# The prologue of a two-layer diffusion backbone in another order: filter network first, modulation tiles between its steps, latent stream and its norm next, context last

## The chip, the core and the metric

The kernel runs on one core of a Trainium2 chip: TensorE (PE) multiplies matrices, VectorE (DVE) and ScalarE (ACT) work on tiles, GpSimd (POOL) and SyncE (SP) mostly issue DMA here. Each engine runs its own list of instructions in order, and they meet only at semaphores. The metric is the device time of one execution in microseconds. The kernel before takes 2734.34 us (median of 3 runs, 2731.32 to 2734.46).

## The reference

Two layers over 512 latent tokens and 256 context tokens of width 1024. What matters for the change is the start:

```
m  = (silu(c) @ w_mod[l] + b_mod[l])             # nine vectors of 1024: shift, scale, gate x 3
mc = (silu(c_ctx) @ w_mod[l] + b_mod[l])
h  = rmsnorm(x, g_pre) * (1 + m_scale) + m_shift # adaln_in, before every sub-layer
x  = x + 0.5 * m_gate * rmsnorm(swiglu(h), g_post)
# the same on ctx with mc
# filter of the odd layer's long convolution, for 512 positions:
a  = sin(freq * (z @ f0 + fb0)); a = sin(freq * (a @ f1 + fb1)); a = sin(freq * (a @ f2 + fb2))
k  = (a @ f3) * exp(-t * deltas)                 # forward and backward taps
kf = rfft(concat(k_f, 0, k_b reversed), 2 * 512)
```

The filter depends on no token, so its spectrum is made in the prologue, ahead of the first feed-forward block, and is stored to HBM until layer 1 wants it.

## The kernel before

Everything is held as columns of 128 partitions: x is eight tiles of 128x512, the context eight of 128x256. Weights stream through rings of four blocks `raw`, split on the chip into a high part (`split_hi`, ACT) and a low part (`split_lo`, DVE), and each product takes three matmuls (`three`, L451 to L453): the bulk of the kernel. The first feed-forward block reads h in the same two parts, `h_hi` and `h_lo`.

The order of the work is written out by hand, engine by engine; nothing reorders it. Four strands run in the prologue:

- **The filter network.** `hidden(0..2)`: a matmul on PE (L477), a chain of DVE operations that reduce the argument (L1371 to L1377), a sine on ACT (L904). Then `make_taps`: eight pairs of matmuls (L490), each result multiplied by a decay table `taper` on DVE (L1327); the tables come in a ring of four, issued by SP.
- **The transforms.** `filter_part(0..11)` on PE, four matmuls each (L503), all on tap tiles that `make_taps` must have finished; ACT copies one half out (`copy_odd`, L910), DVE combines the halves (`make_part`, L1338 to L1342). Part n waits until the combination of part n-2 is done. SP stores each finished pair, 1 MB, to HBM.
- **The modulation tiles.** Groups 0 and 1 (shift and scale of the first sub-layer), eight tiles of 512 KB each, through a ring of four issued by POOL: a slot's next load goes out when PE has used it (`mod_units`, L460). `mod_copy` on DVE takes a finished group out of PSUM, `mod_turn` on PE transposes it, `mod_finish` on DVE adds the bias.
- **The norms.** ACT squares tiles (`square_x`), DVE adds them (`add_square`), PE sums over partitions (`norm_sums`), ACT takes the root, DVE inverts (`norm_root`), PE spreads the result over a bank (`norm_spread`).

Last, `adaln_in` makes the eight h tiles. Per tile d: DVE multiplies x by the spread root (`prod`), ACT scales it (`full`) and rounds it (`h_hi`), DVE subtracts (`h_lo`). Between two tiles both engines run a `beside(d)`, with a transform's copy and combination, and at two places a split of weight block 0 or 1. So tile d and a transform are serial with each other: DVE's prod, ACT's full, h_hi and next `copy_odd`, DVE's next `make_part`, DVE's next prod.

Of the kernel before, what the change touches and what calls it, by code (L numbers as in the profile page):

```python
# [25 lines left out]
KT = D // P  # L26
SEQ = 512
CTX = 256
# [19 lines left out]
PAIRS = 8  # L48
# [66 lines left out]
def build(nc, io):  # L115
# [35 lines left out]
    with ExitStack() as ctx:  # L151
# [226 lines left out]
        def _(sp):  # L378
# [5 lines left out]
            for q in range(PAIRS):  # L384
                if q >= 4:
                    sp.wait_ge(taps_ready, 2 * (q - 3))
                sp.dma_start(taper[:, q % 4], io["decay"][q]).then_inc(taper_landed[q % 4], 16)
                if q == 3:
                    sp.dma_start(x[:], io["x"]).then_inc(x_loaded, 16)
                    sp.dma_start(dft_f[:], io["dft_f"]).then_inc(dft_landed, 16)  # L390

            def load_block(b, rel, first, src):
# [49 lines left out]
        def _(pe):  # L442
# [28 lines left out]
            def hidden(layer):  # L471

                if layer == 0:
                    pe.wait_ge(hid_landed, 16 * 3)
                else:
                    pe.wait_ge(hid_ready, layer)
                pe.matmul(psum[:, 0, :], hid_w[:, layer, :], hid[:, :] if layer else pos[:, :],  # L477
                          start=True, stop=True).then_inc(hid_sum, 1)
# [143 lines left out]
            def first_ffns():  # L622

                sx, sc = ffns[0:2]
                at["h"] += KT
                gate_up(sx[0], SEQ)
                down(sx[1], SEQ, HALF_TILES[0])
                gate_up(sx[2], SEQ)
                down(sx[3], SEQ, HALF_TILES[1])
                norm_sums(SEQ, 1)  # L630
                at["h"] += KT
                g = at["group"]

                def beside(i):
                    if i == 0:
                        norm_spread(SEQ)
                    elif i in (1, 2):
                        mod_units(g, range(4 * i - 4, 4 * i))
                    elif i == 4:
                        mod_turn(g)  # L640
                gate_up(sc[0], CTX, beside)
                at["group"] += 1
                norm_sums(SEQ, 0, CTX_STAT)

                def spread(i):
                    if isinstance(i, int) and i == 0:
                        norm_spread(SEQ)
                down(sc[1], CTX, HALF_TILES[0], spread)
                gate_up(sc[2], CTX)
                down(sc[3], CTX, HALF_TILES[1])  # L650
# [1 line left out]
            pe.wait_ge(zeroed, 3)  # L652
            hidden(0)
            pe.wait_ge(c_ready, 1)
            mod_units(0, range(4))
            hidden(1)
            mod_units(0, range(4, 8))
            hidden(2)
            pe.wait_ge(loaded, 16 * LOADS)
            norm_sums(CTX, 1)  # L660
            make_taps(range(4))
            norm_spread(CTX)
            mod_turn(0)
            mod_units(1, range(4))
            make_taps(range(4, PAIRS))
            filter_part(0)
            mod_units(1, range(4, 8))
            filter_part(1)
            filter_part(2)
            mod_turn(1)  # L670
            filter_part(3)
            norm_sums(SEQ, 1)
            filter_part(4)
            norm_spread(SEQ)
            for n in range(5, PARTS):
                filter_part(n)
            at["group"] = 2
            first_ffns()

# [204 lines left out]
        def _(act):  # L884
# [87 lines left out]
            def adaln_in(T, layer, i, who, hi, beside=lambda d: None):  # L972
                for d in range(KT):
                    beside(d)
                    adaln_tile(T, layer, i, who, hi, d)
                at["pre"] += 1
# [57 lines left out]
            for dst, src in ((ident, "ident"), (b_mod, "b_mod"), (g_pre, "g_pre"), (g_post, "g_post"), (rot, "rot"),  # L1034
                             (head_ones, "head_ones"), (sink, "sink"), (ret, "ret")):
                act.dma_start(dst[:], io[src]).then_inc(loaded, 16)
            act.dma_start(cx[:], io["ctx"]).then_inc(ctx_loaded, 16)
            act.wait_ge(zeroed, 3)
            act.wait_ge(c_loaded, 16)
            act.activation(c_silu[:, :, 0:2], c_cols[:], ACT.Silu).then_inc(c_ready, 1)  # L1040
            hidden(0)
            hidden(1)
            act.wait_ge(ctx_loaded, 16)
            square_x(cx, CTX, None)
            hidden(2)
            norm(CTX)
            act.wait_ge(x_loaded, 16)
            for n, tiles in enumerate((range(2), range(2, 5), range(5, 7), range(7, 8))):
                square_x(x, SEQ, None, tiles)
                copy_odd(n)  # L1050
            norm(SEQ)
            copy_odd(4)

            def beside(d):
                if d < 7:
                    copy_odd(5 + d)
                if d in (4, 5):
                    split_hi(d - 4, 0, 1024)
            adaln_in(SEQ, 0, 0, 0, h_hi, beside)
            act.wait_ge(filt_ready, PARTS)  # L1060
            for d in range(3):
                act.wait_ge(filt_stored[d], 32)
# [220 lines left out]
        def _(dve):  # L1283
# [249 lines left out]
            def first_ffns():  # L1533

                sx, sc = ffns[0:2]
                gate_up(sx[0], SEQ)
                down(sx[1], SEQ, False)
                gate_up(sx[2], SEQ)

# [51 lines left out]

            hidden(0)
            hidden(1)
            for d in range(KT - 1):
                add_square(d, CTX, d)
            hidden(2)
            mod_copy(0)
            make_taps(range(PAIRS))
            norm_root(CTX)
            dve.wait_ge(loaded, 16 * LOADS)  # L1600
            make_taps(range(PAIRS, 2 * PAIRS))
            mod_finish(0, 0, 0)
            dve.wait_ge(rbc_ready, 1)
            seq(dve.tensor_copy(kept_rinv[:, 0:CTX], psum[:, RBC, 0:CTX]))
            for n, tiles in enumerate((range(3), range(3, 5), range(5, 7), ())):
                make_part(n)
                for d in tiles:
                    add_square(KT + d, SEQ, d)
                if n == 1:
                    mod_copy(1)  # L1610
            norm_root(SEQ)
            mod_finish(1, 0, 1)
            make_part(4)
            at["group"] += 2
            gain_pre(0, 0)
            at["step"] += 1
            dve.wait_ge(dve_step, at["step"])
            dve.wait_ge(rbc_ready, 2)

            def beside(d):  # L1620
                if d < 7:
                    make_part(5 + d)
                if d in (5, 6):
                    split_lo(d - 5, 0, 1024)
            adaln_in(x, SEQ, h_hi, h_lo, None, beside)
            dve.wait_ge(filt_ready, PARTS)
            first_ffns()

            def split_ahead(b):
# [493 lines left out]
```

## Time and profile before

| what | us |
|---|---|
| median of 3 runs | 2734.34 |
| the profiled execution | 2735.59 |
| its span in the trace | 2733.9 |
| PE busy in the span | 2504.0 |
| first feed-forward matmul starts | 113.67 |
| last transform's combination starts (DVE) | 111.03 |

The profile is one execution. Its page gives busy time for each engine, then the span in slices, then the chain of waits that ended last, and groups of instructions by line.
### The profile page before, as it was taken

How to read it: one execution, taken by the hardware profiler on the slowest of the kernel's cores; microseconds unless marked ns; L12 is line 12 of the kernel's file. 1: busy time of each engine (PE TensorE's matmuls, PEld its weight loads, DVE VectorE, ACT ScalarE, POOL GpSimd, SP SyncE). 2: the span in 40 equal slices, each digit the busy share in tenths (PEclk: the TensorE clock that was granted, in tenths of full speed). 3: DMA queues.
4: the chain of work that ended last, by engine and by line, in shares of the span. 5: the costliest groups of instructions: out<-in, count | busy, mean ns of one | idle time of the engine just before them, and what ended most of it. 6: DMA issues, size and time to landing. Idle time of an engine off the chain costs nothing.

```text
span 2733.9 us, 32899 instructions
## 1 busy us (share of the span) xinstructions
PE 2504.0 (92%) x12514; PEld 1971.3 (72%) x12514; DVE 1209.1 (44%) x1765; ACT 876.5 (32%) x1283; POOL 111.7 (4%) x186
## 2 busy tenths in 40 slices
PE   5899999999899887899999989999989828899997
PEld 2477788899778434778877778778878527788886
DVE  4523233565553676543222353323355385533334
ACT  1422222444431456343222242222244302422222
POOL 1011000000000110000011000100000000000000
PEclk9999999999999899889999989999979969799999
DMA  7566322455312000132356312552212113132322
GB/s 289 196 219 226 128 96 75 151 176 183 130 62 83 31 1 1 62 108 85 100 200 224 130 58 93 193 181 94 91 55 93 70 46 107 49 102 81 108 77 77
DMA packets 91167, 309.53 MB, mean 113 GB/s; under 512 B 10960, under 2 KB 11632, under 8 KB 89776
## 3 DMA queue, kind: packets, MB, share of 16 engines
q1 hardware_dynamic: 67824, 221.75, 24.2%
q0 software_dynamic: 21936, 84.88, 8.7%
q8 instruction: 75, 1.23, 0.2%
q10 hardware_dynamic: 1296, 1.38, 0.1%
q14 instruction: 36, 0.29, 0.0%
HBM read 299.58 MB, written 8.39 MB: 113 GB/s over the span
## 4 chain that ended last, share of the span: by engine, by line
PE 81%; DVE 8%; ACT 4%; DMA 2%; issue 2%; POOLq 0%; POOL 0%; DVEq 0%; ACTq 0%
PE psum L451 24%; PE psum L452 23%; PE psum L453 23%; PE psum L582 2%; DMA mod_raw<-in_w_mod 2%; PE psum L460 2%; PE psum L873 1%; DVE spectrum L359 1%; DVE term L352 1%; PE psum L740 1%; PE psum L604 1%; DVE w_lo L1297 1%; PE psum L862 1%; DVE stats L1767 1%; ACT w_hi L893 0%
## 5 line engine op out<-in xcount | busy, mean ns | idle before, releaser
L451 PE MATMUL psum<-h_hi,w_hi 128*128 128x512 f32 (+1 forms) x2256 | 860.4, 381 | 28.4 <-DVE h_lo L1480 13.7
L452 PE MATMUL psum<-h_lo,w_hi 128*128 128x512 f32 (+1 forms) x2256 | 848.4, 376 | 0.0
L453 PE MATMUL psum<-h_hi,w_lo 128*128 128x512 f32 (+1 forms) x2256 | 847.5, 376 | 0.0
L451 PEld LDWEIGHTS psum<-h_hi,w_hi 128*128 128x128 f32 x2256 | 429.3, 190 | 128.1 <-issue 35.1
L1297 DVE TENSOR_TENSOR w_lo<-raw,w_hi 128x1024 fp32r<-128x1024 f32 (+2 forms) x442 | 470.6, 1100 | 65.3 <-ACT w_hi L893 61.4
L893 ACT ACTIVATE w_hi<-raw 128x1024 fp32r<-128x1024 f32 (+2 forms) x442 | 405.8, 951 | 251.2 <-PE psum L453 243.7
L453 PEld LDWEIGHTS psum<-h_hi,w_lo 128*128 128x128 f32 x2256 | 429.1, 190 | 77.2
L452 PEld LDWEIGHTS psum<-h_lo,w_hi 128*128 128x128 f32 x2256 | 429.8, 191 | 74.0 <-issue 1.0
L451 PE MATMUL psum<-act_hi,w_hi 128*128 128x512 f32 (+1 forms) x880 | 331.5, 377 | 7.5 <-DVE w_lo L1297 5.5
L453 PE MATMUL psum<-act_hi,w_lo 128*128 128x512 f32 (+1 forms) x880 | 329.2, 374 | 0.0
L452 PE MATMUL psum<-act_lo,w_hi 128*128 128x512 f32 (+1 forms) x880 | 329.1, 374 | 0.0
L1391 DVE TENSOR_TENSOR prod<-psum,square 128x512 f32<-128x512 f32 (+1 forms) x110 | 70.2, 638 | 565.5 <-PE psum L453 560.0
L923 ACT ACTIVATE act_hi<-prod 128x512 f32 (+3 forms) x110 | 64.8, 589 | 550.4 <-DVE prod L1391 550.4
L451 PEld LDWEIGHTS psum<-act_hi,w_hi 128*128 128x128 f32 x880 | 166.9, 190 | 44.5 <-issue 13.1
L453 PEld LDWEIGHTS psum<-act_hi,w_lo 128*128 128x128 f32 x880 | 166.8, 190 | 32.0
L452 PEld LDWEIGHTS psum<-act_lo,w_hi 128*128 128x128 f32 x880 | 167.0, 190 | 31.2
L921 ACT ACTIVATE square<-psum 128x512 f32<-128x512 f32 (+1 forms) x110 | 60.7, 552 | 245.2 <-PE psum L453 245.1
L1938 POOL DMA_DIRECT2D mod_raw<-in_w_mod x144 | 76.4, 530 | 1235.0 <-PE psum L460 1095.8
L1434 DVE COPY y<-psum 128x512 f32<-128x512 f32 (+3 forms) x40 | 25.5, 638 | 195.7 <-PE psum L453 195.6
L1396 DVE TENSOR_TENSOR act_lo<-prod,act_hi 128x512 f32 (+3 forms) x110 | 70.3, 639 | 91.7 <-ACT act_hi L923 91.7
L460 PE MATMUL psum<-mod_raw,c_silu 128*32 128x256 f32 x1152 | 82.3, 409 | 27.3 <-DMA mod_raw<-in_w_mod 25.1
L460 PEld LDWEIGHTS psum<-mod_raw,c_silu 128*32 128x32 f32 x1152 | 31.2, 113 | 73.1 <-DMA mod_raw<-in_w_mod 39.6
(229 smaller groups left out, 1812.5 us busy)
## 6 DMA issues: line engine op xcount, KB each, us to landing
raw<-in_gate_up SPq DMA_DIRECT2D x220, 512.0 KB, 4.2
mod_raw<-in_w_mod POOLq DMA_DIRECT2D x144, 512.0 KB, 5.6
raw<-in_down_a SPq DMA_DIRECT2D x80, 384.0 KB, 3.5
raw<-in_down_b SPq DMA_DIRECT2D x80, 320.0 KB, 3.0
raw<-in_hy_in SPq DMA_DIRECT2D x24, 512.0 KB, 3.5
raw<-in_mix_in SPq DMA_DIRECT2D x22, 512.0 KB, 3.5
filt_dram<-made SPq DMA_DIRECT2D x6, 1024.0 KB, 3.8
filt<-filt_dram POOLq DMA_DIRECT2D x2, 3072.0 KB, 10.9
```

The source lines that it names most:

```text
L451: pe.matmul(out, w_hi[:, slot, c:c + P], hi, start=start, stop=False)
L452: pe.matmul(out, w_hi[:, slot, c:c + P], lo, start=False, stop=False)
L453: return pe.matmul(out, w_lo[:, slot, c:c + P], hi, start=False, stop=stop)
L460: ins = pe.matmul(psum[32 * j:32 * j + 32, MODP, 0:256], c_silu[:, k, :], mod_raw[:, k % RING, 256 * j:256 * j + 256], start=(k == 0), sto ...
L582: ins = pe.matmul(psum[:, bank, t:t + 1], src[:, t * P:t * P + P], ones[:, 0:1], start=first and t == 0, stop=last and t == T // P - 1)
L893: act.activation(w_hi[:, slot, 0:cols], raw[:, slot, 0:cols], ACT.Copy).then_inc(hi_split, 1)
L921: act.activation(silu[:, j, 0:T], psum[:, bank, 0:T], ACT.Silu).then_inc(silu_ready, 1)
L923: act.activation(act_hi[:, bass.ds(2 * i + j, 1), 0:T], prod[:, j:j + 1, 0:T], ACT.Copy).then_inc(act_hi_ready, 1)
L1297: ins = dve.tensor_tensor(w_lo[:, slot, 0:cols], raw[:, slot, 0:cols], w_hi[:, slot, 0:cols].bitcast(F32), ALU.subtract)
L1391: ins = dve.tensor_tensor(prod[:, j, 0:T], psum[:, bank, 0:T], silu[:, j, 0:T], ALU.mult)
L1396: dve.tensor_tensor(act_lo[:, fl, 0:T], prod[:, j:j + 1, 0:T], act_hi[:, fl, 0:T].bitcast(F32), ALU.subtract).then_inc(act_ready, 1)
L1938: pool.dma_start(mod_raw[:, k % RING, :], io["w_mod"][layer, v, k]).then_inc(mod_landed[k % RING], 16)
```

## The change

The same operations run in another order in the prologue:

- PE: two modulation tiles, not four, stand ahead of each network layer; the first taps follow directly on the third layer; the other tiles of group 0 stand between tap pairs. The context's norm sums move from ahead of the taps to behind all transforms, and its spread into the first block of the first feed-forward stage. `mod_turn(1)` stands ahead of transform 2 and no longer behind it; the latent norm's sums stand behind transform 2 and not 3.
- ACT: the context's load is issued after the second sine, not at the start; its squares, formerly between the second and third sine, are made one a tile beside the h tiles; the latent squares come as 2, 4, 2 between the copies.
- DVE: the context's additions go beside the h tiles; `mod_copy(1)` follows all seven latent additions. The h tiles stand beside transforms 4 to 11 (before: 5 to 11), and the splits of blocks 0 and 1 one or two tiles earlier.
- SP: x is issued behind the second decay table, not the fourth.

```diff
@@ SP
                 sp.dma_start(taper[:, q % 4], io["decay"][q]).then_inc(taper_landed[q % 4], 16)
+                if q == 1:
+                    sp.dma_start(x[:], io["x"]).then_inc(x_loaded, 16)
                 if q == 3:
-                    sp.dma_start(x[:], io["x"]).then_inc(x_loaded, 16)
                     sp.dma_start(dft_f[:], io["dft_f"]).then_inc(dft_landed, 16)
@@ PE, first feed-forward stage and prologue
+                def spread_ctx(i):
+                    if isinstance(i, int) and i == 0:
+                        norm_spread(CTX)
+                gate_up(sx[0], SEQ, spread_ctx)
-            mod_units(0, range(4))
+            mod_units(0, range(2))
             hidden(1)
-            mod_units(0, range(4, 8))
+            mod_units(0, range(2, 4))
             hidden(2)
+            make_taps(range(2))
+            mod_units(0, range(4, 6))
+            make_taps(range(2, 4))
+            mod_units(0, range(6, 8))
+            make_taps(range(4, 6))
             pe.wait_ge(loaded, 16 * LOADS)
-            norm_sums(CTX, 1)
-            make_taps(range(4))
-            norm_spread(CTX)
             mod_turn(0)
             mod_units(1, range(4))
-            make_taps(range(4, PAIRS))
+            make_taps(range(6, PAIRS))
             filter_part(0)
             mod_units(1, range(4, 8))
             filter_part(1)
+            mod_turn(1)
             filter_part(2)
-            mod_turn(1)
+            norm_sums(SEQ, 1)
             filter_part(3)
-            norm_sums(SEQ, 1)
-            filter_part(4)
             norm_spread(SEQ)
-            for n in range(5, PARTS):
+            for n in range(4, PARTS):
                 filter_part(n)
+            norm_sums(CTX, 1)
@@ ACT
-            act.wait_ge(ctx_loaded, 16)
-            square_x(cx, CTX, None)
+            act.dma_start(cx[:], io["ctx"]).then_inc(ctx_loaded, 16)
             hidden(2)
-            norm(CTX)
...
             def beside(d):
-                if d < 7:
-                    copy_odd(5 + d)
-                if d in (4, 5):
-                    split_hi(d - 4, 0, 1024)
+                copy_odd(4 + d)
+                square_x(cx, CTX, None, range(d, d + 1))
+                if d in (2, 3):
+                    split_hi(d - 2, 0, 1024)
             adaln_in(SEQ, 0, 0, 0, h_hi, beside)
+            norm(CTX)
@@ DVE
-            for n, tiles in enumerate((range(3), range(3, 5), range(5, 7), ())):
+            for n, tiles in enumerate((range(4), range(4, 7))):
                 make_part(n)
                 for d in tiles:
-                    add_square(KT + d, SEQ, d)
-                if n == 1:
-                    mod_copy(1)
+                    add_square(d, SEQ, d)
+            mod_copy(1)
+            make_part(2)
             norm_root(SEQ)
...
             def beside(d):
-                if d < 7:
-                    make_part(5 + d)
-                if d in (5, 6):
-                    split_lo(d - 5, 0, 1024)
+                if d < KT:
+                    make_part(4 + d)
+                if d in (3, 4):
+                    split_lo(d - 3, 0, 1024)
+                if 1 <= d < KT:
+                    add_square(KT + d - 1, CTX, d - 1)
```

Where that puts things. TensorE's list, from the second network layer to the transforms (L477, L478: network layer; L460, L461: modulation tiles; L490, L491: taps; L503, L504: transforms), before:

```order
L477 MATMUL psum<-hid,hid_w 128x512
L460 MATMUL psum<-mod_raw,c_silu 32x256 x16
L477 MATMUL psum<-hid,hid_w 128x512
L582 MATMUL psum<-ones,sumsq 128x1 x2
L582 MATMUL psum<-ones,square 128x1 x2
L490 MATMUL psum<-f,hid 128x512 x8
L604 MATMUL psum<-ident,full 128x128 x2
L468 MATMUL psum<-ident,mod_row 128x128 x2
```

and now:

```order
L478 MATMUL psum<-hid,hid_w 128x512
L461 MATMUL psum<-mod_raw,c_silu 32x256 x8
L478 MATMUL psum<-hid,hid_w 128x512
L491 MATMUL psum<-f,hid 128x512 x4
L461 MATMUL psum<-mod_raw,c_silu 32x256 x8
L491 MATMUL psum<-f,hid 128x512 x4
L461 MATMUL psum<-mod_raw,c_silu 32x256 x8
```

Two modulation tiles (x8) stand between the layers where four (x16) stood, and the context's sums (L582) and spread (L604) are gone from here.

VectorE's list around transform 1, from its combination (L1338 and L1342, now L1344 and L1348) on; L1414 and L1420 add squares, L1309 and L1315 are `mod_copy(1)`, which TensorE's `mod_turn(1)` waits for. Before:

```order
L1338 TENSOR_TENSOR made<-psum,raw 128x512
L1342 SCALAR_TENSOR_TENSOR made<-psum,raw 128x512
L1414 TENSOR_TENSOR sumsq<-sumsq,square 128x512 x2
L1309 COPY mod_row<-psum 128x256
L1338 TENSOR_TENSOR made<-psum,raw 128x512
```

and now:

```order
L1344 TENSOR_TENSOR made<-psum,raw 128x512
L1348 SCALAR_TENSOR_TENSOR made<-psum,raw 128x512
L1420 TENSOR_TENSOR sumsq<-sumsq,square 128x512 x3
L1315 COPY mod_row<-psum 128x256
L1344 TENSOR_TENSOR made<-psum,raw 128x512
```

Three additions stand ahead of the copy where two stood.

VectorE's list beside two h tiles that have no split, before:

```order
L1338 TENSOR_TENSOR made<-psum,raw 128x512
L1340 TENSOR_TENSOR made<-psum,raw 128x512
L1476 TENSOR_TENSOR prod<-x,psum 128x512
L1480 TENSOR_TENSOR h_lo<-full,h_hi 128x512
L1338 TENSOR_TENSOR made<-psum,raw 128x512
```

and now:

```order
L1344 TENSOR_TENSOR made<-psum,raw 128x512
L1346 TENSOR_TENSOR made<-psum,raw 128x512
L1420 TENSOR_TENSOR sumsq<-sumsq,square 128x256
L1482 TENSOR_TENSOR prod<-x,psum 128x512
L1486 TENSOR_TENSOR h_lo<-full,h_hi 128x512
L1344 TENSOR_TENSOR made<-psum,raw 128x512
```

One addition of 128x256, of the context's squares, now stands between the combination and the next tile's prod.

## Rows read from the trace of the kernel before

**Rows 1.** Part 1 of the page: busy us, share, instructions.

```profile
PE 2504.0 (92%) x12514; PEld 1971.3 (72%) x12514; DVE 1209.1 (44%) x1765; ACT 876.5 (32%) x1283; POOL 111.7 (4%) x186
```

**Rows 2.** Chain of waits near its first matmul: start us, us, what.

```profile
111.03 0.69 DVE made L1338
...
112.32 1.15 DVE w_lo L1297
```

**Rows 3.** Timeline of TensorE, prologue: start us, us, line, tiles, idle before.

```profile
15.38 1.08 PE L460 MATMUL psum<-mod_raw,c_silu 128*32 128x256 f32 x8 [1.53 <-DMA mod_raw<-in_w_mod]
16.39 2.08 PE L477 MATMUL psum<-hid,hid_w 128*128 128x512 f32 x2
...
31.60 1.08 PE L460 MATMUL psum<-mod_raw,c_silu 128*32 128x256 f32 x8 [1.31 <-DMA mod_raw<-in_w_mod]
32.61 2.08 PE L477 MATMUL psum<-hid,hid_w 128*128 128x512 f32 x2
...
39.90 6.26 PE L490 MATMUL psum<-f,hid 64*128 64x512 f32 x16 [4.32 <-ACT hid L904]
...
58.94 3.67 PE L503 MATMUL psum<-taps,dft_f 128*128 128x512 f32 x8 [1.46 <-DVE taps L1327]
62.55 1.93 PE L460 MATMUL psum<-mod_raw,c_silu 128*32 128x256 f32 x32
64.41 7.13 PE L503 MATMUL psum<-taps,dft_f 128*128 128x512 f32 x16
71.92 0.44 PE L468 MATMUL psum<-ident,mod_row 128*128 128x128 f32 x2 [0.38 <-DVE mod_row L1309]
...
75.63 0.95 PE L582 MATMUL psum<-ones,sumsq 128*128 128x1 f32 x8
...
77.33 3.68 PE L503 MATMUL psum<-taps,dft_f 128*128 128x512 f32 x8
80.85 1.05 PE L604 MATMUL psum<-ident,full 128*128 128x128 f32 x8
81.74 17.34 PE L503 MATMUL psum<-taps,dft_f 128*128 128x512 f32 x40
...
113.67 0.76 PE L451 MATMUL psum<-h_hi,w_hi 128*128 128x512 f32 x1 [6.66 <-DVE w_lo L1297]
...
126.15 1.93 PE L460 MATMUL psum<-mod_raw,c_silu 128*32 128x256 f32 x32
```

**Rows 4.** Timeline of ScalarE: a network layer's sine, the first split after the filter.

```profile
11.61 0.63 ACT L904 ACTIVATE hid<-hid_arg_t 128x512 f32<-128x512 f32 x1 [2.35 <-DVE hid_arg_t L1377]
...
121.35 2.01 ACT L893 ACTIVATE w_hi<-raw 128x1024 fp32r<-128x1024 f32 x2 [4.42 <-DMA filt_dram<-made]
```

**Rows 5.** Windows: busy us by engine, granted clock, DMA share, GB/s.

```profile
12.00:17.00 5.00, 2.70 (x17) 0.90 (x18) 0.00 (x0) 0.23 (x1) 0.97 (x2) 1.00 1.04 416
...
114.00:116.00 2.00, 2.00 (x6) 1.52 (x6) 1.66 (x4) 1.88 (x3) 0.00 (x0) 0.50 0.96 252
1070.00:1080.00 10.00, 6.26 (x46) 3.94 (x48) 7.54 (x18) 5.45 (x11) 0.00 (x0) 1.00 0.01 2
```

**Rows 6.** Timeline of VectorE, prologue.

```profile
53.81 4.99 DVE L1327 TENSOR_TENSOR taps<-psum,taper 128x512 f32<-128x512 f32 x8 [5.61 <-PE psum L490]
...
68.85 0.69 DVE L1338 TENSOR_TENSOR made<-psum,raw 128x512 f32<-128x512 f32 x1 [2.25 <-ACT raw L910]
...
71.45 0.42 DVE L1309 COPY mod_row<-psum 128x256 f32<-128x256 f32 x1
...
86.10 0.69 DVE L1338 TENSOR_TENSOR made<-psum,raw 128x512 f32<-128x512 f32 x1 [2.92 <-ACT raw L910]
...
90.07 0.69 DVE L1338 TENSOR_TENSOR made<-psum,raw 128x512 f32<-128x512 f32 x1 [2.08 <-issue]
...
111.03 0.69 DVE L1338 TENSOR_TENSOR made<-psum,raw 128x512 f32<-128x512 f32 x1 [1.48 <-issue]
```

**Rows 7.** VectorE groups by shape: busy us, mean ns.

```profile
L1414 DVE TENSOR_TENSOR sumsq<-sumsq,square 128x256 f32<-128x256 f32 x6 | 2.5, 425 | 0.6
```

More of the change, by code:

```diff
@@ L625, in first_ffns @@
                 at["h"] += KT
-                gate_up(sx[0], SEQ)
+                def spread_ctx(i):
+                    if isinstance(i, int) and i == 0:
+                        norm_spread(CTX)
+                gate_up(sx[0], SEQ, spread_ctx)
                 down(sx[1], SEQ, HALF_TILES[0])
@@ L1036, in _ @@
                 act.dma_start(dst[:], io[src]).then_inc(loaded, 16)
-            act.dma_start(cx[:], io["ctx"]).then_inc(ctx_loaded, 16)
             act.wait_ge(zeroed, 3)
@@ L1042, in _ @@
             hidden(1)
-            act.wait_ge(ctx_loaded, 16)
-            square_x(cx, CTX, None)
+            act.dma_start(cx[:], io["ctx"]).then_inc(ctx_loaded, 16)
             hidden(2)
-            norm(CTX)
             act.wait_ge(x_loaded, 16)
-            for n, tiles in enumerate((range(2), range(2, 5), range(5, 7), range(7, 8))):
+            for n, tiles in enumerate((range(2), range(2, 6), range(6, 8))):
                 square_x(x, SEQ, None, tiles)
@@ L1051, in _ @@
             norm(SEQ)
-            copy_odd(4)
+            copy_odd(3)
+            act.wait_ge(ctx_loaded, 16)
             def beside(d):
-                if d < 7:
-                    copy_odd(5 + d)
-                if d in (4, 5):
-                    split_hi(d - 4, 0, 1024)
+                copy_odd(4 + d)
+                square_x(cx, CTX, None, range(d, d + 1))
+                if d in (2, 3):
+                    split_hi(d - 2, 0, 1024)
             adaln_in(SEQ, 0, 0, 0, h_hi, beside)
+            norm(CTX)
             act.wait_ge(filt_ready, PARTS)
@@ L1535, in first_ffns, with keep_ctx @@
                 sx, sc = ffns[0:2]
-                gate_up(sx[0], SEQ)
+                def keep_ctx(i, j):
+                    if isinstance(i, int) and i == 0 and j == 1:
+                        dve.wait_ge(rbc_ready, 2)
+                        seq(dve.tensor_copy(kept_rinv[:, 0:CTX], psum[:, RBC, 0:CTX]))
+                gate_up(sx[0], SEQ, keep_ctx)
                 down(sx[1], SEQ, False)
@@ L1593, in _ @@
             hidden(1)
-            for d in range(KT - 1):
-                add_square(d, CTX, d)
             hidden(2)
+            make_taps(range(10))
             mod_copy(0)
-            make_taps(range(PAIRS))
-            norm_root(CTX)
+            make_taps(range(10, 2 * PAIRS))
             dve.wait_ge(loaded, 16 * LOADS)
-            make_taps(range(PAIRS, 2 * PAIRS))
             mod_finish(0, 0, 0)
-            dve.wait_ge(rbc_ready, 1)
-            seq(dve.tensor_copy(kept_rinv[:, 0:CTX], psum[:, RBC, 0:CTX]))
-            for n, tiles in enumerate((range(3), range(3, 5), range(5, 7), ())):
+            for n, tiles in enumerate((range(4), range(4, 7))):
                 make_part(n)
                 for d in tiles:
-                    add_square(KT + d, SEQ, d)
-                if n == 1:
-                    mod_copy(1)
+                    add_square(d, SEQ, d)
+            mod_copy(1)
+            make_part(2)
             norm_root(SEQ)
             mod_finish(1, 0, 1)
-            make_part(4)
             at["group"] += 2
             gain_pre(0, 0)
+            make_part(3)
             at["step"] += 1
             dve.wait_ge(dve_step, at["step"])
-            dve.wait_ge(rbc_ready, 2)
+            dve.wait_ge(rbc_ready, 1)
             def beside(d):
-                if d < 7:
-                    make_part(5 + d)
-                if d in (5, 6):
-                    split_lo(d - 5, 0, 1024)
+                if d < KT:
[4 more added lines that the diff above has]
+                    add_square(KT + d - 1, CTX, d - 1)
             adaln_in(x, SEQ, h_hi, h_lo, None, beside)
             dve.wait_ge(filt_ready, PARTS)
+            norm_root(CTX)
             first_ffns()
```

## The prediction

> **What bounds the kernel now.** I read the page's engine totals first, then the chain of waits, then the timelines of TensorE, VectorE and ScalarE over the first 126 us. The totals say that TensorE is busy for 92% of the span [rows 1], so what the change can give is what it takes from the time before TensorE's steady work, or adds to it. The change touches only that stretch: the first feed-forward matmul stands at 113.67 us, after 6.66 us in which TensorE waited for VectorE [rows 3], and the chain of waits runs back from it through the split of block 1 into the combination of the last transform at 111.03 [rows 2]. Behind the first pair of blocks comes the list of before, so each microsecond by which that matmul comes earlier is a microsecond of the kernel, as long as nothing that it needs later is late.
>
> Four pieces set the 113.67. (a) The filter network: layer 1 enters TensorE at 16.39 and layer 2 at 32.61, both behind modulation tiles that waited for their DMA (the tiles before them are at 15.38 and 31.60), and taps start at 39.90 [rows 3]. (b) Taps until the first transform, 39.90 to 58.94 [rows 3]. (c) Transforms 0 to 4, TensorE almost without a gap, until transform 5 at 81.74 [rows 3]. (d) A loop between ScalarE and VectorE: the combination of transform 5 starts at 86.10 and of transform 6 at 90.07, the last at 111.03 [rows 6]. One transform of TensorE lasts about 3.5 us (81.74 plus 17.34 for five) [rows 3], the loop's step 3.97, so here TensorE waits for VectorE.
>
> **(a) The network, cheaper by 13.0 us.** Layer 0's sine ends at 11.61 + 0.63 = 12.24 [rows 4]. Only tiles 0 and 1 stand ahead of layer 1 now, so it enters at 12.3. From a layer's matmul to what follows it takes 39.90 - 32.61 = 7.3 us [rows 3]: layer 2 enters at 19.6. Tiles 2 and 3 in between ended at 15.38 + 1.08 = 16.46 [rows 3] and hide. Taps start at 26.9, against 39.90.
>
> **(b) Taps, to transform 0 at 44.6 (before 58.94).** TensorE starts them after some 5 us of idling. The window behind the wait before the first feed-forward matmul shows the granted clock at 0.50, the level of 1.2 GHz, after 6.66 us idle [rows 3, 5]; eight tap matmuls (four pairs) took 6.26 us from 39.90 [rows 3] with such a start, 1.6 us a pair. I take 1.7 us for each of the first two pairs and half of that later: pairs 0 and 1 until 30.3, tiles 4 and 5 until 31.4, pairs 2 and 3 and tiles 6 and 7 until 34.1. What ends last is the DMA of group 1. Its first four tiles can only go out as slots come free, at 31 to 34, and decay tables 4 to 7 go out as VectorE uses 0 to 3, from 30. That is 8 x 0.5 MB at 416 GB/s, the rate of a full window [rows 5]: about 10 us, until 40.5 or 41. Then pairs 6 and 7 until 42.7, and VectorE's last multiplications at 4.99 / 8 = 0.62 us each [rows 6] until 44.5. If no tile were late it would be 42.7; with 3 us more of DMA, 47.5. I keep both ends. The decay tables 2 and 3 now stand behind x in SP's list; they have until 32 to land, and x and they are part of the bytes already counted.
>
> **(c) Transforms 0 to 3 and the norm, dearer by 6.** Transform 0 until 48.2 (62.55 - 58.94 = 3.6), four tiles until 50.1 (64.41 - 62.55), transform 1 until 53.65 (3.55 each from the pair of 7.13) [rows 3]. Then TensorE stands before `mod_turn(1)`. Before, transform 1 ended at 67.97 under transform 2, its combination began at 68.85, and the copy at 71.45 was through at 71.87 [rows 6], 3.9 us after; the wait in front of the turn was 0.38 because transform 2 covered it [rows 3]. Now that cover is gone, and a third addition, at the 0.75 us of an addition and a squaring that wait for each other (estimate from the 68.85 and 71.45 rows: 2.60 less 1.20 of combination, over two), makes it 4.65: the turn is at 58.3, transform 2 at 58.6. Queued behind that wait is all of TensorE's list. After an idle stretch of that length I expect the clock at 1.2 GHz again; the first seven feed-forward matmuls after 113.67 ran at 0.50 [rows 5], about 3 us that cost 1.5. Transform 2 ends at 58.6 + 3.5 + 1.5 = 63.6. Bounds of the clock's part: 0, and 3.0 if it falls twice (the stretch before transform 0 is also thin). Then the sums (77.33 - 75.63 = 1.7), transform 3 (80.85 - 77.33 = 3.5) and the spread (81.74 - 80.85 = 0.9) [rows 3], until 69.7. The square root's table must now be loaded here; it falls under transform 3 with its inversion and costs nothing, 3.5 us of cover. From the end of the spread to the combination that opens the loop it was 86.10 - 81.74 = 4.36 [rows 3, 6]: 74.05, 12.05 earlier than 86.10.
>
> **(d) The loop, dearer by 7.4.** Before: six steps in 111.03 - 86.10 = 24.93 [rows 6], five of 3.97 and one with a split in it, 1.13 longer. (The second split came behind the last combination.) Now seven steps: 7 x 3.97 = 27.8; both splits inside, 2.26; and in six of them an addition of the context's squares, which lies between VectorE's combination and prod, so in the loop. It lasts 425 ns [rows 7]; as VectorE's instructions overlap by some 50 ns, 0.38 each, 2.3 together. Sum 32.3: the last combination starts at 106.35, against 111.03. ScalarE's squares and first splits stand where it waits for prod and cost nothing. TensorE needs 3.5 us for a transform and has a step of 4.35, so it does not set the pace.
>
> **The end.** Before, 111.03 to 113.67 is 2.64: combination 1.2, split 1.13, the rest issue [rows 2, 3]. Now the split is gone, and the last context addition (0.38) and `norm_sums(CTX)` stand there, which last half of the 1.7 of the latent ones, at 1.2 GHz perhaps 1.0 in all: 106.35 + 1.2 + 0.4 + 1.0 + 0.15 = 109.1. That is 4.6 earlier. The context's spread now falls into TensorE's full work, two matmuls of the four that took 0.9 [rows 3]: +0.45. What is late next are weight blocks 2 and 3, whose slots the transforms use and whose split waits for the last store: 121.35 was 9.1 us after the last combination's end [rows 2, 4], so 116.7 now, and 3.2 us of splits make it 119.9; the pair of blocks 0 and 1 lasts 126.15 - 113.67 = 12.5 [rows 3] until 121.6. Covered by 1.7, and modulation tiles come between.
>
> **The sum.** -13.0 (a), -1.3 (b, 19.0 to 17.7), +2.3 (c and the transform taken out of it: 27.16 from transform 0 to the loop before, 29.45 now), +7.4 (d), end 0.1, spread +0.45: -4.1 us. The profiled execution took 2735.59, which gives 2731.5; it lies 1.25 above the median of 2734.34, so against that the forecast is 2730.2, 0.15% less. A difference under 0.2%, 5.5 us, is what a measurement here can't tell from none.
>
> **Rivals.**
> 1. *The stall of (c) is smaller or the clock holds.* For it: TensorE has only idled about 4.65 us there, and where DMA lands quickly transform 0 can start at 42.7. Against it: the 0.50 window above. With both, 1.5 + 1.9 more: -7.5, 2726.8.
> 2. *The tiles are late.* Everything in (b) hangs on 4 MB issued in one burst from 30 us on, and tiles 4 to 7 of group 1 have only 7 us. Price: 3 us at transform 0 or in front of transform 1: -1.1, 2733.2. Against it: tables and tiles are what the first 27 us have already loaded at full rate.
> 3. *Slower: TensorE's clock falls in the loop.* The transforms now meet a gap of 0.9 us in each step and of 2.0 in the two with a split; at 1.2 GHz a transform lasts 7 us, more than a step, and TensorE sets the pace. From transform 5 at 73.2, seven of them would end at 122.2 and the first feed-forward matmul would stand at 124.6: +10.9 and the spread, +11.4, 2745.7. It decides from the point at which the low clock lasts for more than four transforms (up to there TensorE's lead covers it). Against it: at 1070 to 1080 us TensorE was busy for 6.26 of 10 us and the granted clock was 1.00 [rows 5]. The Trainium skill, "TensorE: Matmul & The Clock Gate", section "A second HAM failure mode: psum-queue depth-cycling", says that small idle gaps between groups of matmuls, as PSUM banks are cycled, can make the clock swing between its levels; this kernel's loop is of that kind, and by that rule alone this rival would be the forecast. The row at 1070 us speaks against the rule here.
>
> **How the numbers follow.** Forecast 0.60, rival 1 0.18, rival 2 0.12, rival 3 and its half-way forms 0.10. The forecast's own spread, from the ends of (b) (-1.9, +3) and of the clock (-1.5, +1.5), is 2727 to 2734; a good third of it is beyond 5.5 us. So faster 0.60 x 0.37 + 0.18 = 0.40, within 0.2% 0.60 x 0.63 + 0.12 = 0.50, slower 0.10. The range goes to 2725.5 for rival 1 with a run spread of 1.5 us, and to 2735.5 for rival 2 likewise.
>
> **What the changed profile would show.** Layer 1 on TensorE at about 12.3 and layer 2 at 19.6; taps at 26.9; transform 0 at 44.6 behind a DMA wait on modulation tiles; a wait of about 4.65 us before L469 for VectorE's mod_row, and a window of 0.50 after it; the loop's combinations 4.35 us apart (5.5 with a split); the first L452 at 109.1; L605 inside the first stage. A transform 0 after 48, a step over 5 us without a split, or blocks 2 and 3 waited for would make the forecast wrong; so would a stall that transform 2 somehow covers.

## The result: slower by 4.5 us, where 4.1 us less was forecast

| | before | changed |
|---|---|---|
| median, us | 2734.46 (9 runs) | 2738.97 (9 runs) |
| lowest to highest | 2728.05 to 2736.39 | 2737.59 to 2744.85 |
| span of the profiled execution | 2733.9 | 2736.4 |
| first network matmul on TensorE | 5.11 | 4.99 |
| first feed-forward matmul | 113.67 | 118.52 |

The ratio is 1.0022, 95% interval 1.0013 to 1.0031: small, but the interval doesn't reach 1. Single runs of either kernel scatter by 7 or 8 us, so the traces are compared by a mark that the scatter of the rest doesn't touch: the time from the first network matmul to the first feed-forward matmul. It was 108.56 us and is 113.53, 5.0 more, and the medians lie 4.5 apart.

### The profile page after: what moved, and what is told of

The parts are those of the page before. It is cut to its first block, busy times and chain, and to the rows that moved or that the text cites. A ratio compares the mean times of both kernels' runs of the same rounds, so it can differ in the third digit from the quotient of the medians.

```text
span 2736.4 us, 32902 instructions
## 1 busy us (share of the span) xinstructions
PE 2506.0 (92%) x12514; PEld 1971.2 (72%) x12514; DVE 1209.5 (44%) x1765; ACT 875.7 (32%) x1283; POOL 111.7 (4%) x186
## 4 chain that ended last, share of the span: by engine, by line
PE 81%; DVE 8%; ACT 4%; issue 2%; DMA 1%; DVEq 0%; POOLq 0%; POOL 0%; ACTq 0%
PE psum L452 24%; PE psum L453 24%; PE psum L454 24%; PE psum L583 2%; PE psum L461 2%; DMA mod_raw<-in_w_mod 1%; PE psum L880 1%; DVE spectrum L359 1%; DVE term L352 1%; PE psum L747 1%; PE psum L605 1%; PE psum L869 1%; DVE stats L1776 1%; DVE w_lo L1303 0%; ACT w_hi L900 0%
## 5 line engine op out<-in xcount | busy, mean ns | idle before, releaser
L454 PEld LDWEIGHTS psum<-act_hi,w_lo 128*128 128x128 f32 x880 | 166.0, 189 | 31.9
L453 PEld LDWEIGHTS psum<-act_lo,w_hi 128*128 128x128 f32 x880 | 166.1, 189 | 31.3
L1440 DVE COPY y<-psum 128x512 f32<-128x512 f32 (+3 forms) x40 | 25.5, 638 | 195.6 <-PE psum L454 195.6
L461 PE MATMUL psum<-mod_raw,c_silu 128*32 128x256 f32 x1152 | 80.4, 402 | 16.6 <-DMA mod_raw<-in_w_mod 14.4
L880 PE MATMUL psum<-idft,spectrum 128*128 128x256 f32 x128 | 32.1, 418 | 56.0 <-DVE spectrum L359 56.0
```

Source lines behind the costliest of these rows:

```text
L453: pe.matmul(out, w_hi[:, slot, c:c + P], lo, start=False, stop=False)
L454: return pe.matmul(out, w_lo[:, slot, c:c + P], hi, start=False, stop=stop)
L880: ins = pe.matmul(psum[:, 4 + n % 2, i * HB:i * HB + HB], y_f[c][:, i, m, t * P:t * P + P], idft[:, m, :], start=(m == 0), stop=(m == 3))
```

## The profile after

The total work of TensorE is nearly the same, 2506.0 us against 2504.0 [rows 1]:

```profile
PE 2506.0 (92%) x12514; PEld 1971.2 (72%) x12514; DVE 1209.5 (44%) x1765; ACT 875.7 (32%) x1283; POOL 111.7 (4%) x186
```

TensorE's timeline of the changed kernel, columns as in [rows 3]. L478 is the network, L491 taps, L461 modulation tiles, L504 transforms, L469 `mod_turn`, L583 and L605 a norm's sums and spread:

```profile
12.16 2.07 PE L478 MATMUL psum<-hid,hid_w 128*128 128x512 f32 x2 [1.05 <-ACT hid L911]
...
19.36 1.32 PE L478 MATMUL psum<-hid,hid_w 128*128 128x512 f32 x2 [3.05 <-ACT hid L911]
25.90 3.79 PE L491 MATMUL psum<-f,hid 64*128 64x512 f32 x8 [5.22 <-ACT hid L911]
...
33.90 1.99 PE L491 MATMUL psum<-f,hid 64*128 64x512 f32 x8
...
45.15 1.08 PE L461 MATMUL psum<-mod_raw,c_silu 128*32 128x256 f32 x8 [1.42 <-DMA mod_raw<-in_w_mod]
46.16 3.79 PE L491 MATMUL psum<-f,hid 64*128 64x512 f32 x8
51.41 5.10 PE L504 MATMUL psum<-taps,dft_f 128*128 128x512 f32 x8 [1.47 <-DVE taps L1333]
56.44 1.93 PE L461 MATMUL psum<-mod_raw,c_silu 128*32 128x256 f32 x32
58.31 3.70 PE L504 MATMUL psum<-taps,dft_f 128*128 128x512 f32 x8
66.62 0.69 PE L469 MATMUL psum<-ident,mod_row 128*128 128x128 f32 x2 [4.61 <-DVE mod_row L1315]
67.10 5.72 PE L504 MATMUL psum<-taps,dft_f 128*128 128x512 f32 x8
72.66 0.95 PE L583 MATMUL psum<-ones,sumsq 128*128 128x1 f32 x8
...
77.88 1.05 PE L605 MATMUL psum<-ident,full 128*128 128x128 f32 x8
78.77 17.61 PE L504 MATMUL psum<-taps,dft_f 128*128 128x512 f32 x40
...
116.79 1.01 PE L583 MATMUL psum<-ones,sumsq 128*128 128x1 f32 x4 [5.24 <-DVE sumsq L1420]
...
118.52 0.77 PE L452 MATMUL psum<-h_hi,w_hi 128*128 128x512 f32 x1
```

The second and third layers enter at 12.16 and 19.36 and the taps at 25.90, where the forecast had 12.3, 19.6 and 26.9: the 13 us are there (39.90 - 25.90 = 14.0). From 37 us on TensorE waits for one tile of group 1 after another, and uses the fourth at 45.15. The last two tap pairs, forecast to be over at 42.7, start at 46.16 and take 3.79 us, where two pairs at full clock take 1.99 (at 33.90), and transform 0 takes 5.10 instead of 3.67 [rows 3]. It starts at 51.41, 7.5 us before the 58.94 of before: half of the gain is gone there, and the wait that follows takes most of the rest. At 66.62 stands the wait for `mod_row` that the forecast had at 4.65 us: 4.61. Transform 2 behind it takes 5.72.

VectorE, the combinations of transforms 1, 4, 6, 7 and 11 (L1344) and the copy behind the additions (L1315), to be read beside [rows 6]:

```profile
62.74 0.69 DVE L1344 TENSOR_TENSOR made<-psum,raw 128x512 f32<-128x512 f32 x1 [1.49 <-ACT raw L917]
...
66.14 0.42 DVE L1315 COPY mod_row<-psum 128x256 f32<-128x256 f32 x1
...
83.18 0.69 DVE L1344 TENSOR_TENSOR made<-psum,raw 128x512 f32<-128x512 f32 x1 [3.12 <-ACT raw L917]
...
91.33 0.69 DVE L1344 TENSOR_TENSOR made<-psum,raw 128x512 f32<-128x512 f32 x1 [1.48 <-issue]
...
95.63 0.69 DVE L1344 TENSOR_TENSOR made<-psum,raw 128x512 f32<-128x512 f32 x1 [1.48 <-issue]
...
115.11 0.69 DVE L1344 TENSOR_TENSOR made<-psum,raw 128x512 f32<-128x512 f32 x1 [1.48 <-issue]
```

From the combination at 62.74 to the copy at 66.14 it is 3.4 us (2.6 before, one addition less). The step at 91.33 to 95.63 is 4.30 (3.97 before), the loop 115.11 - 83.18 = 31.93 (32.3 forecast).

Five windows of the changed kernel; the last three columns are granted clock, DMA share and GB/s:

```profile
20.00:30.00 10.00, 4.78 (x14) 1.47 (x16) 5.77 (x10) 1.67 (x3) 0.00 (x0) 0.51 1.00 414
30.00:36.00 6.00, 5.88 (x48) 2.10 (x40) 4.40 (x8) 0.00 (x0) 2.11 (x4) 0.97 0.90 298
40.00:50.00 10.00, 6.02 (x28) 1.59 (x24) 1.31 (x3) 0.00 (x0) 1.68 (x4) 0.53 1.02 397
68.00:72.00 4.00, 4.00 (x7) 1.69 (x6) 0.00 (x0) 0.00 (x0) 0.00 (x0) 0.58 0.09 37
100.00:110.00 10.00, 6.53 (x15) 2.50 (x14) 6.78 (x11) 4.73 (x9) 0.00 (x0) 1.00 0.17 70
```

The clock is at 0.51 and 0.53 in the two stretches in which TensorE waits for the network and for tiles, while the DMA engines are full; it is at 0.58 in transform 2; and at 1.00 in the loop, where TensorE is busy for 6.5 of 10 us. So the third rival's fall of the clock did not come. The Trainium skill ("TensorE: Matmul & The Clock Gate", section "A second HAM failure mode: psum-queue depth-cycling") reports of a bf16 kernel that small gaps between groups of matmuls, as PSUM banks are cycled, made the clock swing. This trace does not agree: its fp32 transforms go round four banks too, with gaps of 0.6 to 1.74 us in front of the last three, and the granted clock stays at 1.00.

POOL's issues of group 1's first four tiles, each pair when TensorE has used the slots:

```profile
31.31 1.19 POOL L1947 DMA_DIRECT2D mod_raw<-in_w_mod  x2 [13.79 <-PE psum L461]
34.21 1.19 POOL L1947 DMA_DIRECT2D mod_raw<-in_w_mod  x2 [1.71 <-PE psum L461]
```

They go out at 31.31 to 34.9, as forecast ("at 31 to 34"). The fourth lands 10.2 us later, at 45.1, where the forecast had 41. Between 30 and 36 us the DMA engines are busy (0.90) but move only 298 GB/s, not the 416 that the forecast counted with, and from 31.3 to 45.15 they move 5.1 MB (13.84 us at 371 GB/s), not the 4 that it counted: weight blocks 0 and 1 and the next tiles go out in between.

ScalarE's split of blocks 2 and 3 came at 125.66 against 121.35 [rows 4], the same distance behind the last combination, and was not waited for, as forecast.

## The experiments

All but the last are edits of the changed kernel. "The mark" is the first feed-forward matmul minus the first network matmul in the profiled execution. Each ratio is to the kernel before as timed beside that run, so ratios compare better than medians.

| run | mark, us | median, us | ratio to before, 95% |
|---|---|---|---|
| before | 108.56 | | |
| changed | 113.53 | 2738.97 | 1.0022 [1.0013, 1.0031] |
| turn_behind | 108.80 | 2738.23 | 1.0011 [0.9995, 1.0027] |
| taps_first | 106.86 | 2733.45 | 0.9999 [0.9986, 1.0012] |
| adds_aside | 110.86 | 2740.59 | 1.0012 [0.9996, 1.0028] |
| raw_late | 111.95 | 2735.67 | 1.0013 [1.0000, 1.0026] |
| tiles_early | 105.37 | 2730.65 | 0.9998 [0.9987, 1.0008] |
| filler | 110.17 | (one run) 2736.46 | |
| three | 104.62 | 2730.27 | 0.9995 [0.9985, 1.0006] |
| copy_only | 106.59 | 2732.48 | 0.9988 [0.9977, 1.0000] |
| copy_ahead | 93.07 | 2719.89 | 0.9963 [0.9949, 0.9976] |
| before_copy (edit of before) | 103.61 | 2729.74 | 0.9985 [0.9971, 0.9999] |

**tiles_early: why the tiles were late.**

```diff
             hidden(2)
+            mod_units(0, range(4, 6))
             make_taps(range(2))
-            mod_units(0, range(4, 6))
-            make_taps(range(2, 4))
             mod_units(0, range(6, 8))
+            make_taps(range(2, 4))
             make_taps(range(4, 6))
```

> The changed kernel with tiles 4 and 5 of modulation group 0 used right behind the third network layer (TensorE waits there for 5.2 us anyway) and tiles 6 and 7 behind tap pair 1, so that the ring's slots come free for group 1 some 7 us earlier (they went out at 31.31 to 35.4). Theory G (group 1 was late because its slots came free late): its fourth tile is used at 38 to 40 and no longer at 45.15, and the first feed-forward matmul comes 5 to 6 us earlier. Theory H (the DMA engines were full, so the bytes that had to be moved by then set the time): they were at 0.84 to 0.96 only from 30 to 36 us, so the fourth tile comes 1 to 2 us earlier at most.

POOL's issues for group 1 and TensorE's rows:

```profile
24.07 0.53 POOL L1947 DMA_DIRECT2D mod_raw<-in_w_mod  x1 [5.76 <-PE psum L461]
27.70 0.53 POOL L1947 DMA_DIRECT2D mod_raw<-in_w_mod  x1 [3.10 <-PE psum L461]
33.06 0.53 POOL L1947 DMA_DIRECT2D mod_raw<-in_w_mod  x1 [4.84 <-PE psum L461]
33.90 0.53 POOL L1947 DMA_DIRECT2D mod_raw<-in_w_mod  x1 [0.31 <-issue]
```

```profile
22.31 1.08 PE L461 MATMUL psum<-mod_raw,c_silu 128*32 128x256 f32 x8
25.94 1.08 PE L461 MATMUL psum<-mod_raw,c_silu 128*32 128x256 f32 x8 [2.55 <-DMA mod_raw<-in_w_mod]
...
38.98 1.93 PE L461 MATMUL psum<-mod_raw,c_silu 128*32 128x256 f32 x32
...
44.64 3.67 PE L504 MATMUL psum<-taps,dft_f 128*128 128x512 f32 x8 [1.80 <-DVE taps L1333]
```

A window of this run:

```profile
30.00:36.00 6.00, 5.39 (x30) 1.38 (x28) 3.94 (x7) 0.00 (x0) 1.05 (x2) 1.00 0.99 403
```

Tiles 4 and 5 of group 0 were there at 22.31 and 25.94, inside TensorE's wait for the network; the changed kernel used them only at 29.62. The first two tiles of group 1 go out at 24.07 and 27.70 and not at 31.31 and 32.0, and at 38.98 all four are used in one piece (x32) without a wait. The fourth is through 5.3 us earlier (6.2 counted from the first network matmul), transform 0 starts at 44.64, and the mark falls by 8.2, to 3.2 under that of the kernel before. The clock gives 3.2 of the 8.2: it is high again for the last tap pairs (1.99) and transform 0 (3.67). Theory G holds: late slots made the tiles late. But the fourth tile's own slot was hardly late: it goes out at 33.90, 1 us earlier than in the changed kernel, and lands in 5.9 us instead of 10.2. What the edit took away are two of the loads that stood with it in the burst, and the DMA engines move 403 GB/s from 30 to 36 us instead of 298. Whether the smaller burst or the higher rate counts for more isn't told apart.

**raw_late: were it the bytes?**

```diff
+            sp.wait_ge(filt_ready, 1)
             def load_block(b, rel, first, src):
```

> The changed kernel with the loads of weight blocks 0 and 1 (1 MB) held until the first transform's combination is done; they were issued at 35 to 37 us, in the middle of the burst of decay tables and modulation tiles. Theory A (the bytes of that burst set the landing): 1 MB less at 416 GB/s makes the fourth tile of group 1 land 2.4 us earlier, at 42.7, and all behind it. Rival F (the tiles wait for their ring slots, not for bytes): tile 4 stays at 45.15.

```profile
45.60 1.08 PE L463 MATMUL psum<-mod_raw,c_silu 128*32 128x256 f32 x8 [0.46 <-DMA mod_raw<-in_w_mod]
...
51.43 3.67 PE L506 MATMUL psum<-taps,dft_f 128*128 128x512 f32 x8 [1.47 <-DVE taps L1335]
```

The fourth tile is still used at 45.60; theory A's 42.7 failed. It went out 1.4 us later in this run and landed in 9.3 us instead of 10.2, so holding back that 1 MB gave about 1 us. (From 30 to 36 us the DMA engines moved even less than in the changed kernel, 223 GB/s; why the rate falls there stays open.) The mark's 1.6 comes from a transform 0 at full clock (3.67). Together with tiles_early: what counted was when the tiles went out and what went out with them, not the weight blocks.

**taps_first: what stood behind the tiles.**

```diff
-            mod_units(1, range(4))
             make_taps(range(6, PAIRS))
+            mod_units(1, range(4))
             filter_part(0)
```

> The changed kernel with tap pairs 6 and 7 ahead of the first four tiles of modulation group 1 on TensorE, not behind them. In the changed kernel TensorE waited for those tiles until 45.15, ran the two pairs at a half clock until 49.95, and transform 0 started at 51.41. Theory A (late tiles in front of the last taps): transform 0 starts as soon as the fourth tile is used, at 46.2, so 5 us earlier, and the first feed-forward matmul at 113.3. Rival D (the tiles are not what is late but the decay tables of those pairs): transform 0 stays at 50 or later.

```profile
45.71 0.64 PE L461 MATMUL psum<-mod_raw,c_silu 128*32 128x256 f32 x8 [1.70 <-DMA mod_raw<-in_w_mod]
46.28 3.70 PE L504 MATMUL psum<-taps,dft_f 128*128 128x512 f32 x8
```

The tile is as late as before (45.71), yet transform 0 starts at 46.28, as theory A had it, and the mark falls by 6.7. Both kernels use the tile at about the same time; what is spared is the two tap pairs and VectorE's multiplications behind it, 5.1 us. The rest is the clock (transforms 0 and 2 take 3.70 and 4.76 us, not 5.10 and 5.72), less 1.1 us at the last tile of group 1, which is late in its turn.

**turn_behind: the wait for the copy.**

```diff
             filter_part(1)
-            mod_turn(1)
             filter_part(2)
+            mod_turn(1)
```

> The changed kernel with mod_turn(1) behind transform 2 again, as before the change; nothing else. Its first feed-forward matmul stood at 118.52 us, after a wait of 4.61 us in front of that turn and a transform 2 of 5.72 us at a half clock. Theory A (the gain of the network was spent on three waits ahead of the loop: late tiles, this turn, and the clock that both lower): the wait goes and transform 2 takes about 3.7, so the first feed-forward matmul comes 6 to 7 us earlier, near 112, and the kernel 6 us. Rival B (the loop beside the h tiles alone sets the end, whatever comes ahead of it): it stays within 1 us of 118.5. Rival C (only the clock counts, the wait moves to another place behind transform 1): 2 us earlier.

```profile
58.55 7.13 PE L504 MATMUL psum<-taps,dft_f 128*128 128x512 f32 x16
66.86 0.44 PE L469 MATMUL psum<-ident,mod_row 128*128 128x128 f32 x2 [1.17 <-DVE mod_row L1315]
...
68.83 5.38 PE L504 MATMUL psum<-taps,dft_f 128*128 128x512 f32 x8
```

Transform 2 covers the wait, 1.17 us of it are left, and the mark falls by 4.7. That is less than the 6 to 7 expected: transforms 1 and 2 run at full clock (7.13 for both), but now transform 3 takes 5.38. The low clock has moved behind the norm's sums. From transform 1 to transform 4 this run needs 16.4 us and the changed kernel 20.5: 4.1 us are the edit's. The rest of the 4.7 is transform 0, at full clock here, less tiles that came somewhat later. By their ratios to the kernel before (1.0011 and 1.0022) the two differ by 3 us, within their intervals.

**filler: the clock by itself.**

```diff
+            for _ in range(4):
+                pe.matmul(psum[:, STAT, :], dft_f[:, 0, 0, 0, :], taps[0][:, 0, :], start=True, stop=True)
             mod_turn(1)
```

> The changed kernel with four spare matmuls of a transform's shape (3.4 us, into a bank that nothing reads) in front of mod_turn(1), so that TensorE waits 1.2 us there and not 4.61. It gives the clock's part alone: theory A (the low clock after the wait costs about 2 us in transform 2): transform 2 takes 3.7 and not 5.72, and the first feed-forward matmul comes 2 us earlier although the turn is at the same time. Rival: transform 2 stays at 5 or more, the clock doesn't follow the wait.

```profile
60.91 3.60 PE L677 MATMUL psum<-taps,dft_f 128*128 128x512 f32 x8
65.67 0.44 PE L469 MATMUL psum<-ident,mod_row 128*128 128x128 f32 x2 [1.17 <-DVE mod_row L1317]
65.95 3.60 PE L504 MATMUL psum<-taps,dft_f 128*128 128x512 f32 x8
```

The turn comes no sooner (65.67 - 57.37 from the start of transform 1, 8.30 as in the changed kernel), but transform 2 takes 3.60. From its start to the sums it is 3.44, against 5.56: the low clock cost 2.1 us there, where the forecast had 1.5. That is one pair of profiles: in the five other runs that keep this wait in front of transform 2 (taps_first, adds_aside, raw_late, tiles_early, copy_only), the transform took 4.76 to 6.17 us, so the cost is 1.2 to 2.6. The mark falls by 3.4; the rest is transform 0, at full clock in this run.

**adds_aside: the additions in the loop.**

```diff
-                if 1 <= d < KT:
+                if d == KT - 1:
                     add_square(KT + d - 1, CTX, d - 1)
-            adaln_in(x, SEQ, h_hi, h_lo, None, beside)
+            for d in range(KT + 1):
+                beside(d)
+                adaln_tile(x, SEQ, h_hi, h_lo, psum[:, RBC, 0:SEQ], d)
+                if 1 <= d < KT - 1:
+                    add_square(KT + d - 1, CTX, d - 1)
+            at["pre"] += 1
```

> The changed kernel with six of the seven additions of the context's squares behind h_lo, where VectorE waits 1.48 us a step, and not between the combination and prod. Theory A: the steps of the loop fall from 4.30 to 3.97 us, 1.9 us in all, and the first feed-forward matmul comes at 116.6. Rival B (the loop alone sets the end): the same 1.9 here, but then turn_behind and taps_first give nothing. Rival E (TensorE or ScalarE sets the step): 4.30 stays.

```profile
91.61 0.69 DVE L1344 TENSOR_TENSOR made<-psum,raw 128x512 f32<-128x512 f32 x1 [1.28 <-issue]
...
95.57 0.69 DVE L1344 TENSOR_TENSOR made<-psum,raw 128x512 f32<-128x512 f32 x1 [1.15 <-issue]
```

Steps are 3.96 again. The loop lasts 113.71 - 83.65 = 30.06, 1.9 less, as expected. The mark's other 0.8 is transform 0 at full clock. The median of this run (2740.59) does not follow, its ratio (1.0012 against 1.0022) does; the intervals overlap.

**three: turn_behind, taps_first and adds_aside together.**

> The changed kernel with three of the edits already tried together: mod_turn(1) behind transform 2, tap pairs 6 and 7 ahead of the modulation tiles, six context additions behind h_lo. Counted from the first network matmul (108.56 us to the first feed-forward matmul in the kernel before, 113.53 in the changed one), the three gave 4.7, 6.7 and 2.7 alone. Theory A (three waits in a row on one chain, so their gains add but for the clock's part that two of them share): 11 to 14 less than the changed kernel, about 101, and the kernel 6 to 8 us faster than before. Rival B (one place behind them all sets the end): no more than the best of them, 106.9.

```profile
46.69 1.08 PE L461 MATMUL psum<-mod_raw,c_silu 128*32 128x256 f32 x8 [1.86 <-DMA mod_raw<-in_w_mod]
47.70 5.92 PE L504 MATMUL psum<-taps,dft_f 128*128 128x512 f32 x8
```

A miss of 3 us: the mark is 104.62, not 101. The fourth tile came at 46.69 in this run, and most of transform 0 ran at the low clock (5.92 us; 0.50 from 47 to 51 us), so only 3.0 of the 5.7 us that taps_first gained up to transform 1 were there. It is 4 us under the mark of the kernel before; its time can't be told from that kernel's.

**copy_only and before_copy: the loop's own chain.** The same edit in both kernels, ScalarE's copy one tile ahead:

```diff
             def beside(d):
-                copy_odd(4 + d)
+                if d == 0:
+                    copy_odd(4)
+                if d < KT - 1:
+                    copy_odd(5 + d)
                 square_x(cx, CTX, None, range(d, d + 1))
```

> The changed kernel with only ScalarE's copy of the odd half made one h tile ahead. Theory A (the step of 4.30 us is the chain prod, full, h_hi, copy, combination, addition; the copy's 0.5 us and its hand-over leave it): steps of 3.6 us or a little more, TensorE's 3.5 being the floor, the loop from 31.9 to 27 us, and the first feed-forward matmul 4 to 5 us earlier, at about 109 from the first network matmul, as in the kernel before. Rival (in copy_ahead it was the other edits that shortened the steps): 4.30 stays.

> The kernel before with the same one edit. Theory A: its steps of 3.97 fall to 3.5, about 3 us over six steps, and its first feed-forward matmul comes at 105 to 106 from the first network matmul (108.56 before). Rival (TensorE, at 3.5 plus a gap of 0.27, sets the step there): 1.5 us at most.

Combinations, of copy_only and then of before_copy:

```profile
92.44 0.69 DVE L1347 TENSOR_TENSOR made<-psum,raw 128x512 f32<-128x512 f32 x1 [0.73 <-PE psum L504]
...
95.88 0.69 DVE L1347 TENSOR_TENSOR made<-psum,raw 128x512 f32<-128x512 f32 x1 [0.61 <-issue]
```

```profile
89.92 0.69 DVE L1340 TENSOR_TENSOR made<-psum,raw 128x512 f32<-128x512 f32 x1 [1.51 <-PE psum L503]
...
93.35 0.69 DVE L1340 TENSOR_TENSOR made<-psum,raw 128x512 f32<-128x512 f32 x1 [0.95 <-PE psum L503]
```

Steps of 3.44 and 3.43 us, TensorE's pace. In copy_only the loop lasts 109.61 - 85.67 = 23.94 instead of 31.93; 27 was expected, because I had left the splits in the chain, and they fit into VectorE's slack as well. The mark falls by 6.9. In the kernel before it falls by 5.0, to 103.61, where 105 to 106 was expected: its loop lasts 20.66 us instead of 24.93, 4.3 less and not 3, for the same reason.

**copy_ahead: all of it together** (the edits of three, tiles_early and copy_only).

> The kernel of the label three, with the tile order of tiles_early, and with ScalarE's copy of a transform's odd half made one h tile ahead, so that it is no longer between h_hi and VectorE's next combination. Theory A (the loop's step is the serial chain prod, full, h_hi, copy, combination): the step falls from 3.97 to TensorE's 3.5, 3 us over the loop, first feed-forward matmul at about 97 from the first network matmul. Rival (TensorE's wait for the combination two back sets the step): 3.97 stays.

```profile
67.47 27.63 PE L504 MATMUL psum<-taps,dft_f 128*128 128x512 f32 x64
97.50 0.60 PE L583 MATMUL psum<-ones,sumsq 128*128 128x1 f32 x4 [2.40 <-DVE sumsq L1423]
```

Eight transforms without a gap (x64, 27.63 us), the mark at 93.07, 4 us lower than expected, and the kernel 10 us faster than before, ratio 0.9963, interval 0.9949 to 0.9976. Its loop is that of copy_only, its fourth tile waits for nothing; it beats both kernels.

## Why the prediction was wrong

Its steps, measured by the same marks:

| step | forecast | measured |
|---|---|---|
| (a) taps start | 26.9 | 25.90 |
| (b) from there to transform 0 | 17.7 | 25.5 |
| (c) to the combination that opens the loop | 29.45 | 31.8 |
| (d) the loop | 32.3 | 31.9 |
| the end, to the first feed-forward matmul | 2.75 | 3.4 |
| first feed-forward matmul | 109.1 | 118.52 |
| the context's spread | 0.45 | 0.54 |

- **(a) was right.** The network no longer waits for tiles. The 1 us under the forecast is a third layer that ran partly at full clock (1.32 us).
- **(b) failed, and it is the step that turned the sign.** The term that failed is the landing of group 1's first four tiles: I set it by bytes (8 x 0.5 MB at 416 GB/s, until 41) and took +3 us as the upper end; (b) came out 7.8 over. Of these, 6.2 are the tiles (the fourth is through at 46.16, 20.3 behind the start of the taps, 14.1 forecast) and 2.1 the tap pairs behind them at half clock, which I had put at full clock, less 0.5 at the tail. The times at which the tiles go out were right (31 to 34 forecast, 31.31 to 34.9 measured); the landing took 10.2 us for the last of them, at 298 GB/s from 30 to 36 us and with 5.1 MB moved instead of 4. tiles_early shows what the forecast took as given: the edit that freed the network parked tiles 4 and 5 behind tap pairs that wait for the same network, so the first two loads of group 1 went out 7.2 and 4.3 us later than in that run, into the burst of decay tables that the same taps release. taps_first shows the second half: whatever stands behind a late tile in TensorE's list is late too. My second rival named late tiles, but priced them at 3.
- **(c) had the wait right and the clock short.** 4.61 us for 4.65. The clock's part was 2.1 behind it (filler), not 1.5, and another 1.4 in transform 0, which I had put only at the upper end.
- **(d) was right**, in the step of 4.30 (4.35 forecast) and the sum; an addition cost 0.33 us, not 0.38, and the first of the six is a cheaper copy. What I didn't ask is whether ScalarE's copy had to be in the chain. It hadn't, in either kernel.
- **The end** was 0.65 longer, because the sums ran at a low clock: 118.52 - 116.79 = 1.73 for 1.0. In copy_ahead, at a clock of 1.00, they took 98.42 - 97.50 = 0.92.
- The third rival (the clock falls in the loop) and the rival at 2726.8 did not happen. The kernel was slower by another road than the one that I had priced for it: the four steps and the end together are 9.4 us over the forecast, and without the 7.8 of (b) the first feed-forward matmul would still have come earlier than before.

## What to carry to other kernels

A ring of buffers that a consumer frees in its own order turns each wait of the consumer into a later load: when work is moved ahead of a ring's reader, ask when the slots come free and what else is issued at that time, not only whether the data has landed; a load that goes out in a burst can land later than its bytes at the best rate say (here 10.2 us, with about 7 forecast). Where a loop passes between two engines, look for a copy in the chain that can be made one round ahead of the round that needs it; here that took the step from 4.30 us to 3.44, TensorE's pace. And price a new wait on TensorE at its length plus what the clock takes after it, here 1.2 to 2.6 us on top of 4.6.

## What the runs showed of the hardware

- After thin work the low clock (0.50, 1.2 GHz) cost different amounts at the same place of the same code: transform 0, behind the same tiles and tap pairs, took 5.10 us in the changed kernel and 5.31 in copy_only, but 3.67 in turn_behind, adds_aside, raw_late and filler. The mark of a single profile carries some 1.5 to 2 us of that.
- In turn_behind the transform behind a wait of only 1.17 us and two short rows of norm sums ran low (5.38 us; the same in three and copy_ahead), while transforms with gaps of up to 1.74 us between them never did. A short wait is no promise when the work around it is short as well.
- The marks and the medians agree in sign and roughly in size where the mark moved by more than 4 us (copy_ahead 15.5 and 10.1; the changed kernel 5.0 and 6.0 by their ratios); below that the times don't tell. Of copy_ahead's 15.5, 2.2 are gone again by the modulation tiles at 155.28 us (168.34 in the kernel before): there TensorE waits 4.79 us for a tile (3.89 before), and the context's spread stands in between. So a microsecond at the mark was not quite a microsecond of the kernel; the rest of the difference isn't traced.
